# Columns C and V, and the second half's Fourier and pooling gates, of the first mixing stage as seven block products for eight

## The reference, cut to what matters

```python
h = rmsnorm(x, g_mix[l])
p = h @ w_in[l]                                   # 1024 -> F, B, C, V, P (512 each) and three gates of 1024
gates = sigmoid(p[..., OFF_G:]).reshape(b, s, 3, d)
y_f = fourier_mix(p[F], w_fourier[l])
y_c = short_conv(p[B], p[C], p[V], w_conv[l], w_conv_out[l])     # z = C * V; conv over 3 tokens; (B * conv) @ w_out
y_p = pool_mix(p[P], w_pool[l], pool_scale[l])
merged = gates[0] * y_f + gates[1] * y_c + gates[2] * y_p
x = x + merged @ w_o[l]
```

## Time and profile before

| what | value |
|---|---|
| median of 3 runs | 2215.58 us |
| the profiled execution, its own time | 2217.72 us |
| its span | 2215.9 us |
| busy in the span: TensorE, VectorE, ScalarE | 100%, 78%, 60% |
| granted TensorE clock | 1.0 |
| mean HBM traffic | 227 GB/s |

### The profile page before, as it was taken

How to read it: one execution, slowest core, us unless ns; L and a number is a source line. 1 busy time by engine, 2 the same in 40 slices (tenths; PEclk the granted TensorE clock), 3 DMA queues, 4 the chain that set the end, 5 groups by cost and what they waited for, 6 DMA issues and landing times.

```text
span 2215.9 us, 28791 instructions
## 1 busy us (share of the span) xinstructions
PE 2208.1 (100%) x11494; PEld 1886.2 (85%) x11494; DVE 1729.2 (78%) x2163; ACT 1321.5 (60%) x1489; POOL 56.0 (3%) x68
## 2 busy tenths in 40 slices
PE   9999999999999999999999999999999999999999
PEld 8888888888888888888888888888888888788887
DVE  7887566888788566788888799768788887976787
ACT  6566445556556544666656676555565667754555
POOL 0000000000000000000000000000000000000000
PEclk9999999999999999999999999999999999999999
DMA  7977555977879556698597753549778785345876
GB/s 274 327 224 259 166 185 186 310 224 234 287 245 273 187 172 208 215 300 236 193 321 239 236 171 118 204 160 325 231 234 277 239 261 195 105 162 195 287 244 185
DMA packets 170950, 503.86 MB, mean 227 GB/s; under 512 B 18720, under 2 KB 23328, under 8 KB 162624
## 3 DMA queue, kind: packets, MB, share of 16 engines
q1 hardware_dynamic: 161456, 434.90, 55.1%
q0 software_dynamic: 9216, 67.11, 15.4%
q10 hardware_dynamic: 144, 0.00, 0.0%
HBM read 500.91 MB, written 1.05 MB: 227 GB/s over the span
## 4 chain that ended last, share of the span: by engine, by line
PE 90%; DVE 4%; DMA 4%; ACT 1%; issue 1%; SPq 0%; ACTq 0%; DVEq 0%
PE psum L756 24%; PE psum L757 12%; PE psum L692 12%; PE psum L694 12%; PE psum L693 12%; PE psum L888 4%; PE psum L892 4%; PE psum L890 4%; DMA raw<-t_gate_up_1a_dram 2%; DVE split_w L1843 2%; PE psum L724 2%; DMA raw<-t_gate_up_2a_dram 1%; PE psum L1115 1%; DVE gate_up L1983 1%; ACT split_w L1315 0%
## 5 line engine op out<-in xcount | busy, mean ns | idle before, releaser
L1843 DVE TENSOR_TENSOR split_w<-raw,split_w 128x2048 fp32r<-128x2048 f32 (+3 forms) x389 | 842.5, 2177 | 147.4 <-ACT split_w L1315 145.2
L1315 ACT ACTIVATE split_w<-raw 128x2048 fp32r<-128x2048 f32 (+3 forms) x389 | 708.5, 1830 | 291.4 <-PE psum L694 58.4
L756 PE MATMUL psum<-xt,split_w 128*128 128x512 f32 x2464 | 860.1, 393 | 0.5 <-DVE split_w L1843 0.3
L757 PE MATMUL psum<-xt,split_w 128*128 128x256 f32 x2464 | 690.3, 280 | 0.0
L756 PEld LDWEIGHTS psum<-xt,split_w 128*128 128x128 f32 x2464 | 461.2, 187 | 104.0 <-issue 0.6
L757 PEld LDWEIGHTS psum<-xt,split_w 128*128 128x128 f32 x2464 | 465.7, 189 | 0.5
L692 PE MATMUL psum<-split_w,xt 128*128 128x512 f32 (+1 forms) x736 | 289.5, 393 | 0.0
L694 PE MATMUL psum<-split_w,xt 128*128 128x512 f32 (+1 forms) x736 | 283.7, 385 | 0.0
L693 PE MATMUL psum<-split_w,xt 128*128 128x512 f32 (+1 forms) x736 | 283.6, 385 | 0.0
L1983 DVE TENSOR_TENSOR gate_up<-psum,low 128x512 f32<-128x512 f32 x176 | 120.7, 686 | 98.3 <-ACT low L1392 98.1
L692 PEld LDWEIGHTS psum<-split_w,xt 128*128 128x128 f32 x736 | 138.3, 188 | 28.9 <-issue 3.0
(11 more groups left out here) (309 smaller groups left out, 2871.6 us busy)
## 6 DMA issues: line engine op xcount, KB each, us to landing
raw<-w_in_dram SPq DMA_DIRECT2D x180, 512.0 KB, 4.5
raw<-t_gate_up_1b_dram SPq DMA_DIRECT2D x88, 512.0 KB, 6.5
raw<-t_gate_up_2a_dram SPq DMA_DIRECT2D x88, 512.0 KB, 5.9
raw<-t_gate_up_2b_dram SPq DMA_DIRECT2D x88, 512.0 KB, 6.1
raw<-t_gate_up_1a_dram SPq DMA_DIRECT2D x84, 512.0 KB, 6.8
left_sums<-ffn_w_down_quarters_dram POOLq DMA_DIRECT2D x24, 1024.0 KB, 10.0
raw<-ffn_w_down_quarters_dram SPq DMA_DIRECT2D x48, 512.0 KB, 4.4
left_sums<-w_a_quarters_dram POOLq DMA_DIRECT2D x12, 1024.0 KB, 11.0
```

The costliest lines, as they stand in the source:

```text
L756: nc.tensor.matmul(bank, whi[:, slot, w], xt[:, c, :, :], start=c == 0, stop=False)
L757: last = nc.tensor.matmul(bank[:, 0:T], wlo[:, slot, w], xt_hi[:, c, :], start=False, stop=c == DC - 1)
L1315: nc.scalar.activation(whi[:, e.unit(u) % HL, 0:n], raw[:, r, 0:n], ACT.Copy).then_inc(hi_done, 1)
L1843: nc.vector.tensor_tensor(wlo[:, e.unit(u) % HL, 0:n], raw[:, r, 0:n], whi[:, e.unit(u) % HL, 0:n], ALU.subtract).then_inc(w_ready, 1)
```

## The change

C and V are taken as one set, and the columns of the second half's Fourier and pooling gates as another. In a set, the left operand is split in token halves and even and odd input chunks, and the weights in four blocks of 512 x 512 per side ("11", "12", "21", "22"). Seven products (11, U, T2, 21, T3, 22, T4) give the four results. Each is one unit of 1 MB and 12 matmuls; the sums of weight blocks U, T2 and T4 grow in one buffer (`set_left`), T3 in another (`set_right`, which lies where the pooling matrices were). Accumulating DMAs on GpSimd's queue make them, but for the step from U to T2, which VectorE adds from the raw block "22" (`set_sum`). The left operands' sums are made once a stage by VectorE and ScalarE (`token_sums`, `token_sums_lo`). The accumulator in PSUM bank 0 runs on through 11, T2, T3 and T4, and ScalarE copies its state (`e1`, `e2`, `e3`) and U (`u`) to SBUF between them; VectorE then forms the results (`quarter_added`, `quarter_apart`, `snapshots_apart`). B moves ahead of the set, the first half's Fourier gate and product too; the convolution's gate and product of the second half move ahead of the second set, its pooling and Fourier products behind. The stage has 38 units, eight of which (the sums) don't go through `raw`. The diff, cut; of a replaced line only the new one is shown:

```diff
+SETS = ({name: 9 + i for i, name in enumerate(("11", "U", "T2", "21", "T3", "22", "T4"))},
+        {"11": 25, "U": 26, "T2": 27, "21": 28, "T3": 29, "22": 30, "T4": 32})
+SET_SUMS = [units[name] for units in SETS for name in ("U", "T2", "T3", "T4")]
+SUMMED = {"U": 0, "T3": 1, "T2": 2, "22": 3}
+MIX_UNITS = {1: 38, 2: 36}
...
+        def bank_of(name):
+            return 2 if name == "21" else 1 if name in ("U", "22") else 0
...
+                fourier(u0 + 8, 0)
+                for q in ("11", "21", "22"):
+                    set_load(u0 + set_unit(0, q), q, 0)
+                wide(w_in, u0 + 16, OFF_G + 2 * D)
+                pooling(u0 + 18, 0)
+                wide(w_in, u0 + 19, OFF_G + D)
+                convolution(u0 + 21, 0)
+                wide(w_in, u0 + 22, OFF_G + D + 512)
+                convolution(u0 + 24, 1)
+                for q in ("11", "21", "22"):
+                    set_load(u0 + set_unit(1, q), q, 1)
+                pooling(u0 + 31, 1)
+                fourier(u0 + 33, 1)
...
+                def product(n, name):
+                    out = psum[:, bank_of(name), :]
+                    u = u0 + set_unit(n, name)
+                    slot = e.unit(u) % HL
+                    eng.wait_ge(w_ready, units(e, u, RAW))
+                    for i in range(DC // 2):
+                        hi, lo = left(name, i)
+                        w = slice(i * 512, (i + 1) * 512)
+                        start = i == 0 and name in ("11", "U", "21")
+                        stop = i == DC // 2 - 1
+                        nc.tensor.matmul(out, hi, whi[:, slot, w], start=start, stop=False, skip_group_check=True)
+                        nc.tensor.matmul(out, hi, wlo[:, slot, w], start=False, stop=False, skip_group_check=True)
+                        last = nc.tensor.matmul(out, lo, whi[:, slot, w], start=False, stop=stop, skip_group_check=True)
+                    last.then_inc(w_used, 1)
+                def branch_out(u, p, split, n):
+                    blocks(u, 0, p, split, (2 * n, 2 * n + 1), True, True, True, 256, beside=True)
+                def conv_out(u):
+                    blocks(u, 0, 2, (bz_hi, bz_lo), range(4), True, True, True)
+                wide(u0 + 6, 1, XT)
+                eng.wait_ge(acted, e.after(acted, ("tok", "B")))
+                branch_out(u0 + 8, 2, (fq_hi, fq_lo), 0)
+                product(0, "11")
+                eng.wait_ge(done, e.after(done, ("s",)))
+                product(0, "U")
+                eng.wait_ge(acted, e.after(acted, ("e1", 0)))
+                product(0, "T2")
+                eng.wait_ge(acted, e.after(acted, ("sig", 0, "f")))
+                product(0, "21")
+                eng.wait_ge(acted, e.after(acted, ("e2", 0)))
+                product(0, "T3")
+                eng.wait_ge(acted, e.after(acted, ("u", 0)))
+                product(0, "22")
+                eng.wait_ge(acted, e.after(acted, ("e3", 0)))
+                product(0, "T4")
+                eng.wait_ge(done, e.after(done, ("x00", 0)))
+                wide(u0 + 16, 1, XT, 0, 1)
                 eng.wait_ge(done, e.after(done, ("z", 1)))
                 turns("zt", z)
...
+                wide(u0 + 16, 1, XT, 1, 3)
                 eng.wait_ge(acted, e.after(acted, ("zt", 1)))
                 turns("bt", tok)
...
+                product(1, "11")
+                product(1, "U")
+                eng.wait_ge(acted, e.after(acted, ("e1", 1)))
+                product(1, "T2")
+                eng.wait_ge(acted, e.after(acted, ("sig", 1, "c")))
+                product(1, "21")
+                eng.wait_ge(acted, e.after(acted, ("e2", 1)))
+                product(1, "T3")
+                eng.wait_ge(acted, e.after(acted, ("u", 1)))
+                product(1, "22")
+                turns("mt0", ptok)
+                eng.wait_ge(done, e.after(done, ("merged", 1, "c")))
+                branch_out(u0 + 31, 2, (pl_hi, pl_lo), 1)
+                eng.wait_ge(acted, e.after(acted, ("e3", 1)))
+                product(1, "T4")
+                eng.wait_ge(done, e.after(done, ("x00", 1)))
+                branch_out(u0 + 33, 1, (fq_hi, fq_lo), 1)
+                u = u0 + 34
+                eng.wait_ge(done, e.after(done, ("mt0", 1)))
+                eng.wait_ge(done, e.after(done, ("x01", 1)))
                 eng.wait_ge(acted, e.after(acted, ("sig", 1, "f")))
...
+                gate(0, "f", 1, u0 + 7)
+                set_sum_split(0, "T2")
+                split(u0 + 12)
+                snapshot("e1", 0, "11", z[:, 0, :])
+                set_sum_split(0, "T3")
+                snapshot("u", 0, "U", sigs[:, 1, 1, :])
+                split(u0 + 14)
+                snapshot("e2", 0, "T2", sigs[:, 1, 0, :])
+                set_sum_split(0, "T4")
+                split(u0 + 16)
+                snapshot("e3", 0, "T3", sigs[:, 0, 1, :])
+                split(u0 + 17)
+                split(u0 + 18)
+                split(u0 + 19)
...
+                gate(0, "c", 0, u0 + 20)
+                split(u0 + 24)
+                split(u0 + 25)
+                set_sum_split(1, "U")
+                eng.wait_ge(done, e.after(done, ("merged", 0, "c")))
+                gate(1, "c", 1, u0 + 23)
+                set_sum_split(1, "T2")
+                split(u0 + 28)
+                snapshot("e1", 1, "11", sigs[:, 0, 0, :])
+                set_sum_split(1, "T3")
+                snapshot("u", 1, "U", sigs[:, 1, 1, :])
+                split(u0 + 30)
+                snapshot("e2", 1, "T2", sigs[:, 1, 0, :])
+                split(u0 + 31)
+                set_sum_split(1, "T4")
+                snapshot("e3", 1, "T3", sigs[:, 0, 1, :])
+                eng.wait_ge(done, e.after(done, ("wf", 1)))
+                split(u0 + 33)
+                eng.wait_ge(done, e.after(done, ("x00", 1)))
+                sigmoid(sigs[:, 0, 0, :], sigs[:, 0, 0, :], 0)
+                eng.wait_ge(done, e.after(done, ("x11", 1)))
+                sigmoid(sigs[:, 1, 1, :], sigs[:, 1, 1, :], 1)
+                eng.wait_ge(done, e.after(done, ("x01", 1)))
+                sigmoid(sigs[:, 1, 0, :], sigs[:, 1, 0, :], 0).then_inc(acted, e.mark(acted, ("sig", 1, "p")))
+                for j in range(2):
+                    turned_hi(mt1_hi, ("mt0", j), 6 + j, 2 * j)
+                split(u0 + 34)
+                split(u0 + 35)
+                multiplied(u0 + set_unit(1, "T4"))
+                sigmoid(sigs[:, 0, 1, :], psum[:, bank_of("T4"), :], 1).then_inc(
+                    acted, e.mark(acted, ("sig", 1, "f")))
+                split(u0 + 36)
...
+                for n in range(2):
+                    if n == 0:
+                        eng.wait_ge(done, e.after(done, ("s",)))
+                    else:
+                        split_done(0, "T4")
+                    load(set_left, "11", n, set_left_in)
+                    add(set_left, "12", n, set_left_added)
+                    if n == 0:
+                        eng.wait_ge(small, e.after(small, ("pl", 1)))
+                    load(set_right, "12", n, set_right_in)
+                    add(set_right, "22", n, set_right_added)
+                    split_done(n, "T2")
+                    add(set_left, "21", n, set_left_added)
...
+            def set_sum(n):
+                u = FFN_UNITS + set_unit(n, "22")
+                eng.wait_ge(raw_in[e.place(u) % RAW], loaded(e, u))
+                eng.wait_ge(w_ready, units(e, FFN_UNITS + set_unit(n, "U"), RAW))
+                nc.vector.tensor_tensor(set_left[:, :], set_left[:, :], raw[:, e.place(u) % RAW, :],
+                                        ALU.add).then_inc(set_summed, 1)
+            def token_sums():
+                for half in range(2):
+                    eng.wait_ge(done, e.after(done, ("xt", "mix", half, 1)))
+                flat = sigs.rearrange("p b m n -> p (b m n)")
+                e.link(nc.vector.tensor_tensor(rstd_squared[:, :], rstd[:, :], rstd[:, :], ALU.mult))
+                e.link(nc.vector.tensor_tensor(flat.rearrange("p (c t) -> p c t", c=DC), xt_hi, xt_lo, ALU.add))
+                q = flat.rearrange("p (i k t) -> p i k t", k=4, t=P)
+                sa = set_left.rearrange("p (i k t) -> p i k t", k=4, t=P)
+                e.link(nc.vector.tensor_tensor(sa[:, :, 0:2, :], q[:, :, 3:1:-1, :], q[:, :, 1::2, :], ALU.subtract))
+                e.link(nc.vector.tensor_tensor(sa[:, :, 2, :], sa[:, :, 0, :], q[:, :, 2, :], ALU.subtract))
+                nc.vector.tensor_tensor(sa[:, :, 3, :], sa[:, :, 2, :], q[:, :, 0, :], ALU.add).then_inc(
+                    done, e.mark(done, ("sa",)))
+            def token_sums_lo():
+                eng.wait_ge(acted, e.after(acted, ("s",)))
+                nc.vector.tensor_tensor(mt1_lo.rearrange("p c t -> p (c t)"), set_left[:, :],
+                                        mt1_hi.rearrange("p c t -> p (c t)"), ALU.subtract).then_inc(
+                                            done, e.mark(done, ("s",)))
...
```

(87 more changed lines are left out.)

276 lines of the change are left out of this document (133 added, 143 removed).

## The result

Four runs of the changed kernel have a median of 2237.47 us (2235.08 to 2238.74), beside 2216.3 us for four of the kernel before: a ratio of 1.0093, 95% interval 1.0076 to 1.0111. It is slower, 4.2 us above the forecast of 2233.3 and within the range.

What follows compares the result with a forecast made beforehand. TensorE's stream was taken as the bound; per stage, 24 fewer matmuls (-5.4 us), first-set waits (+5.5) and second-set waits (+8.8) gave +8.9, +17.7 for two: 2233.3 us on the median, range 2221 to 2246.

Steps and rivals of the forecast that it cites:

- The rival in which TensorE stays the bound: VectorE's 62 us to spare absorb the added work, and fewer matmuls make the run faster, 2204.7 us; chance 0.12.
- The `w_o` wait: Second set's tail: TensorE waits 3.1 us before `w_o` for the chain ending in the last gate.
- The `mt1` wait: Second set's tail: TensorE waits 5.1 us before the `mt1` transposes for VectorE's pooling branch, unit 35 and Fourier branch.
- 18 matmuls, 4.1 us: Second set's tail: `w_o` runs 18 matmuls in 4.1 us before TensorE needs the merged second half.
- The z wait: First set's end: TensorE waits 2.2 us before the z transposes, behind VectorE's 7.9 us after T4's split.
- The T4 wait: First set's end: TensorE waits 3.3 us before T4, with its last sum landing after the median 11.2 us.
- The feed-forward step of the earlier trace: Same sum step before the change: issued 155.31, taken by ScalarE 164.04; 9.4 us from split's end, with few other loads.
- faster beside little traffic: Sign: a first wait, before T4, under 1 us would mean accumulating loads are faster beside little traffic.
- lands in 4.5 us and is issued at least 10 us ahead: SyncE's ordinary unit loads: landing takes 4.5 us, issue is at least 10 us ahead.
- conv: The wait before the convolution product in the second half; the prediction named no wait there.
- Half clock: Rival: each 5 us wait is followed by a half-clock stretch costing 5.4 us more, 2244 us in all; chance 0.08.
- the small wait at the end: Within the second half's blocks: unit 36's split, ahead of the transposed remainders, adds 0.6 us.

Runs made afterwards that it cites:

- g1: Changed kernel without the second set: only C and V as seven products, second half's gates back to plain units in the old order; 2218.32 us, 1.0007 of before.
- e3: Changed kernel with the second set's tail reordered: folding ahead of results, unit 34 earlier, units 35 and 36 later; 2224.28 us, 1.003 of before.
- e2: Changed kernel with GpSimd's loads for the second set begun when unit 20 is split, not at the first T4's split; 2240.22 us, 1.0107 of before.
- g3: Both sets with e3's tail order, T2 ahead of the first gate, and GpSimd's second-set loads from unit 19's split on; 2219.49 us, 1.0016 of before.
- e4: Changed kernel with unused matmuls filling TensorE's tail gaps, 12 ahead of `w_o` and 16 ahead of `mt1`; 2233.56 us, 1.0074 of before.
- h1: g1 with z ahead of units 17 and 18, T2's rounding ahead of the Fourier gates, `e1` ahead of unit 12's rounding; 2215.27 us, 0.9991 of before.
- i1: h1 with one tiny unused sigmoid on ScalarE ahead of T2's rounding, so the table loads in idle time; 2211.9 us, 0.9983 of before.

## Why the prediction was right, and where not

**The mechanism held.** Two chains on VectorE, ScalarE and GpSimd's queue, one behind the first set's last sum and one behind the second set's last results, cost more than 24 matmuls a stage give. g1 and e3 show it from both sides: without the second set the run is at 2218.3, with it but another tail at 2224.3. VectorE's and ScalarE's added work itself was hidden, as costed (130 us busy). The rival in which TensorE stays the bound needed `w_o` and `mt1` without a wait; they wait 2.9 and 3.1 or more.

**The `w_o` wait**, forecast 3.1: 2.92 in both stages.

**The `mt1` wait**, forecast 5.1: 3.35 and 3.13. The chain was right. The timeline of VectorE after:

```profile
342.06 0.68 DVE L2409 TENSOR_TENSOR part<-psum,sigs 128x512 f32<-128x512 f32 x1
...
346.41 2.29 DVE L2018 TENSOR_TENSOR split_w<-raw,split_w 128x2048 fp32r<-128x2048 f32 x1
348.62 0.68 DVE L2409 TENSOR_TENSOR part<-psum,sigs 128x512 f32<-128x512 f32 x1
...
350.79 0.69 DVE L2413 TENSOR_TENSOR merged<-merged,part 128x512 f32<-128x512 f32 x1
```

From 342.06 to 351.48 are 9.4 us, against 4.35 + 2.2 + 2.9 = 9.45 in the step. What failed is the term "18 matmuls, 4.1 us": they ran in part at half clock and took 5.6 and 5.8, which hid 1.5 and 1.7 of the wait. In e2's first stage they ran at full clock behind the same 2.92, and `mt1` waited 4.72.

**The z wait**, forecast 2.2: 1.88 and 1.84.

**The T4 wait**, forecast 3.3 from a landing at the median: 1.07 and 0.83. The timelines of GpSimd, then ScalarE and VectorE:

```profile
246.89 0.88 POOL L1979 DMA_DIRECT2D set_left<-w_in_quarters_dram  x1 [8.68 <-DVE split_w L2033]
```

```profile
255.35 1.92 ACT L1431 ACTIVATE split_w<-set_left 128x2048 fp32r<-128x2048 f32 x1 [3.14 <-DMA set_left<-w_in_quarters_dram]
```

```profile
257.30 2.29 DVE L2033 TENSOR_TENSOR split_w<-set_left,split_w 128x2048 fp32r<-128x2048 f32 x1 [2.65 <-ACT split_w L1431]
```

The issue follows T2's split (end 246.45) by 0.4 us, forecast 0.6, and ScalarE takes the block 8.5 us after the issue, inside the 7.7 to 14.8 of the earlier trace rows but not at its median of 10.6. The feed-forward step of the earlier trace rows, 8.7 from issue to ScalarE, was the nearer row. The prediction set it aside as one "with few other loads", which misread it: the DMA engines are 97% busy there (155.3 to 164.04), and 81% from 246.9 to 255.3 here. So the sign "faster beside little traffic" has no support, though the second stage's wait is under 1 us.

**The step that was missing.** The prediction dismissed SyncE's loads: "lands in 4.5 us and is issued at least 10 us ahead". The 4.5 is a median over the whole run, most of it without GpSimd's loads beside it; SyncE's loads issued from 255 to 275 landed after 5.4 to 15.4 us, median 10.7. Timelines of GpSimd, ScalarE and VectorE after:

```profile
259.97 0.55 POOL L1975 DMA_DIRECT2D set_left<-w_in_quarters_dram  x1 [12.20 <-DVE split_w L2033]
265.40 0.86 POOL L1979 DMA_DIRECT2D set_left<-w_in_quarters_dram  x1 [4.87 <-DMA set_left<-w_in_quarters_dram]
```

```profile
269.01 1.92 ACT L1410 ACTIVATE split_w<-raw 128x2048 fp32r<-128x2048 f32 x1 [7.14 <-DMA raw<-w_in_dram]
...
279.73 1.92 ACT L1410 ACTIVATE split_w<-raw 128x2048 fp32r<-128x2048 f32 x1 [7.84 <-DMA raw<-w_in_dram]
```

```profile
289.50 2.29 DVE L2018 TENSOR_TENSOR split_w<-raw,split_w 128x2048 fp32r<-128x2048 f32 x1
291.71 1.28 DVE L2487 TENSOR_TENSOR bz_lo<-cv,bz_hi 128x512 fp32r<-128x512 f32 x2
```

ScalarE idles twice for units from SyncE, VectorE's pooling branch and unit 21 follow late, and `bz_lo` is queued behind them: conv waits 3.27. e2 shows the cause (later loads, no conv wait), g1 and g3 too. Its size is not set by the order. Timelines of SyncE and ScalarE after, both stages:

```profile
261.82 3.68 SPq L524 DMA_DIRECT2D raw<-w_in_dram  x4
...
804.43 3.68 SPq L524 DMA_DIRECT2D raw<-w_in_dram  x4
```

```profile
819.33 1.92 ACT L1410 ACTIVATE split_w<-raw 128x2048 fp32r<-128x2048 f32 x1 [5.55 <-DMA raw<-w_in_dram]
```

Units 19 and 20 are issued alike in both, 2.1 to 5.8 us after T4's first matmul (259.74 and 802.34), but ScalarE takes unit 20 20.0 us after it in the first stage and 17.0 in the second. These 3.0 us are the difference of the two conv waits. In e3 and e4, unchanged around this product, the waits are 2.07 and 0.82, 1.83 and 2.29. What makes the same loads land sooner or later stays open.

**Half clock**, a rival with 0.08, came true in part. Its price, 5.4 us behind each `mt1` wait, was too high: the stretches cost 1.3 to 1.7 each, and those behind `w_o` vanish in the wait that follows. By e4 0.9 us of the run were the tail's; that the stretch behind conv cost its 1.3 was not tried apart.
The rule of the Trainium skill (TensorE: Matmul & The Clock Gate, Part 1) that idle time brings the throttle back was borne out here by the windows at 0.72 and 0.77, though not behind each wait.

In sum, measured less forecast, first and second stage: T4 and z -2.6 and -2.8, `w_o` -0.2 twice, `mt1` -1.8 and -2.0, the small wait at the end -0.6 and -0.2; conv +3.3 and +0.3, half clock and refilling +5.6 and +3.0. That is +3.7 and -1.9 on the +8.9 forecast for each. So 2233.3 stands close to 2237.5 partly by luck, because errors cancelled.

## What to carry to other kernels

Trading matmuls for chained results is paid at the places where the next product needs the last result: price that chain from the result on, instruction by instruction in the order of each queue, and only then compare it with what TensorE saves; an engine's mean slack (62 us here) says nothing about it. Before giving such a trade up, reorder the queues around the chain, which was worth some 12 of 21 us here, and cut it to the part whose chain fits. When a step is moved, look at what else it releases (a split frees a load's buffer) and at what the first instruction of its kind drags along (a table load).

## What the runs showed of the hardware

- The granted clock fell to half for some 3 us after idle times of 2.92 us (both stages), 3.27 and 3.35, and in e3 after 2.07 (conv, first stage) and 2.12 (`mt1`, second), but not after one of 3.13 in the changed kernel, 2.92 in e2 (`w_o`, first stage) or 2.16 in e3; the length of the idle time alone doesn't decide it. With the tails' gaps filled (e4) it stayed at 1.00 there. Behind the waits that end at 293.10 and 880.43 the first 1.0 and 0.8 us still ran at full clock.
- A sigmoid's table load takes 1.28 us and stands where the first sigmoid after other functions stands, though ScalarE idles for 4.75 us one instruction ahead (h1); a tiny sigmoid there moved it into the idle time (i1).
- An accumulating load of 1 MB was taken 8.5 us after its issue with the DMA engines 81% busy. Ordinary loads beside GpSimd's left ScalarE idle for 7 to 8 us; before, the longest such wait in the stage was 3.86. The same loads, issued alike, were taken 3.0 us apart in the two stages.
